# Four modulation rows computed by VectorE beside the first projections, and their own stage left out

## The reference, cut to what matters

```python
sh1, sc1, gt1, sh2, sc2, gt2 = split(silu(c) @ w_mod + b_mod, 6)
p = modulate(x, norm1_g, sh1, sc1) @ w_in          # first projections: q, k, v of the attention, and more
o_da = diff_attn(rope(q), rope(k), v)
o_gdn = gated delta rule, both directions
x_new = x + gt1 * (concat(o_da, o_gdn) @ w_out)
h = rms_norm(x_new, norm2_g) * (1 + sc2) + sh2      # router and experts work on h
x_new = x_new + gt2 * experts(h)
```

## Time and profile before

| | us |
|---|---|
| median of 3 runs | 4340.51 (4334.54 to 4346.90) |
| the profiled execution, its own time | 4332.25 |
| its span, first to last instruction | 4330.4 |
| TensorE (PE) busy | 3777.9 |
| VectorE (DVE) busy | 1570.3 |
| ScalarE (ACT) busy | 762.6 |
| GpSimd (POOL) busy | 310.4 |

### The profile page before, as it was taken

How to read it: one execution, slowest core, us unless ns; L and a number is a source line. 1 busy time by engine, 2 the same in 40 slices (tenths; PEclk the granted TensorE clock), 3 DMA queues, 4 the chain that set the end, 5 groups by cost and what they waited for, 6 DMA issues and landing times. The chain is left out here.

```text
span 4330.4 us, 32749 instructions
## 1 busy us (share of the span) xinstructions
PE 3777.9 (87%) x12890; PEld 1994.8 (46%) x12890; DVE 1570.3 (36%) x2513; ACT 762.6 (18%) x1409; POOL 310.4 (7%) x260
## 2 busy tenths in 40 slices
PE   7989989777798399999959476888888999999999
PEld 3446664446645144444435353344443444444444
DVE  3226634566413500000142617899812132121000
ACT  2014423333401000000020114122220110010000
POOL 0000000034200000000010000000000022121000
PEclk8999989888898699999979757889999999999999
DMA  5000000052352488888650101101122201110211
GB/s 180 20 21 1 1 2 29 30 133 58 122 195 78 172 337 320 313 322 312 243 187 0 12 10 52 39 22 30 37 92 97 97 30 49 39 49 20 83 58 44
DMA packets 193501, 425.97 MB, mean 98 GB/s; under 512 B 71648, under 2 KB 119936, under 8 KB 180672
## 3 DMA queue, kind: packets, MB, share of 16 engines
q1 hardware_dynamic: 183936, 392.57, 26.1%
q0 software_dynamic: 8272, 29.38, 2.3%
q10 hardware_dynamic: 1152, 2.10, 0.1%
HBM read 374.78 MB, written 48.05 MB: 98 GB/s over the span
## 5 line engine op out<-in xcount | busy, mean ns | idle before, releaser
L1728 PE MATMUL psum<-arena 128*128 128x512 f32 x1536 | 670.0, 594 | 2.9 <-DVE arena L1811 1.3
L2842 PE MATMUL psum<-arena 128*128 128x512 f32 x1232 | 532.4, 595 | 5.7 <-DVE arena L2900 4.1
L1728 PEld LDWEIGHTS psum<-arena 128*128 128x128 f32 x1536 | 289.4, 190 | 360.8 <-issue 357.8
L2842 PEld LDWEIGHTS psum<-arena 128*128 128x128 f32 x1232 | 234.7, 191 | 302.8 <-issue 294.6
L2498 PE MATMUL psum<-arena 128*128 128x512 f32 x512 | 264.6, 664 | 75.1 <-ACT arena L2571 75.0
L2969 PE MATMUL psum<-arena 128*128 128x512 f32 x704 | 305.0, 596 | 7.9 <-DMA arena<-in_w_ffn_down_dram 7.5
L2969 PEld LDWEIGHTS psum<-arena 128*128 128x128 f32 x704 | 133.8, 190 | 179.0 <-issue 170.6
L677 PE MATMUL psum<-arena 128*128 128x512 f32 (+1 forms) x512 | 202.2, 551 | 1.1 <-PEq L396 1.1
L2498 PEld LDWEIGHTS psum<-arena 128*128 128x128 f32 x512 | 102.4, 211 | 213.5 <-issue 189.7
L2610 DVE MAX8 arena<-arena 128x8 f32<-128x1024 f32 (+5 forms) x192 | 171.2, 892 | 4.7
L2612 DVE MATCH_REPLACE8 arena<-arena 128x1024 f32<-128x1024 f32 (+5 forms) x192 | 168.5, 878 | 0.0
(11 more groups left out here) (456 smaller groups left out, 4642.1 us busy)
## 6 DMA issues: line engine op xcount, KB each, us to landing
arena<-in_w_gate_dram SPq DMA_DIRECT2D x32, 2048.0 KB, 7.3
arena<-in_w_up_dram SPq DMA_DIRECT2D x32, 2048.0 KB, 8.8
arena<-in_w_down_dram SPq DMA_DIRECT2D x32, 2048.0 KB, 7.9
arena<-in_w_mod_dram SPq DMA_DIRECT2D x12, 2048.0 KB, 12.3
arena<-gd_rows SPq DMA_DIRECT2D x56, 256.0 KB, 4.2
arena<-in_w_ffn_gate_dram SPq DMA_DIRECT2D x11, 1024.0 KB, 5.5
arena<-in_w_ffn_up_dram SPq DMA_DIRECT2D x11, 1024.0 KB, 5.3
arena<-in_w_ffn_down_dram SPq DMA_DIRECT2D x22, 512.0 KB, 3.7
```

Of the source, the lines that this page charges most:

```text
L1728: ins = nc.tensor.matmul(ps[:, banks + j, :], lhs[:, k], W[n][:, h, k % 4, j * 512:(j + 1) * 512], start=(k == 0), stop=(k == KD - 1))
L2842: ins = nc.tensor.matmul(out(q), left[:, k], right[:, k], start=first and k == 0, stop=last and k == 3, skip_group_check=not first)
```

## The change

The eight chunks of the four rows are computed in stage_da_project. SyncE loads w_mod's chunks there into a ring of two (w_rows). After each rotary step r VectorE runs row_part(r): four of the eight 128x512 slices of chunk r // 2, each multiplied by its column of silu_c and added into acc (one tensor_scalar or scalar_tensor_tensor each). The sum over the 128 partitions is left to TensorE: row_sum(c), one product of acc with a matrix of ones, into bank 6 or 7, right after the swap of step 2c + 3 (the last one before the last task). VectorE copies one partition of it (row_out), and SyncE stores it as 2 KB in DRAM (mod_rows). stage_gdn_out now loads the four rows (2 MB), their biases (2 MB) and norm2_g (0.5 MB) as broadcasts to 128 partitions after the gate, and then w_out; GpSimd adds the biases and makes the scale row, in three operations of 4096, 1024 and 1024 elements a partition. stage_rows is dropped from the list.

```diff
--- before.py
+++ after.py
@@ -286,6 +286,11 @@
     raw = A.take("raw", 3, 512)
     tmp = A.take("rope_tmp", 2, 512)
     w_in = e.in_["w_in"][0].rearrange("(k p) n -> p k n", p=P)
+    NC = 8
+    wm, acc, row = A.take("w_rows", 2, KD, 512), A.take("row_acc", 2, 512), A.take("row_out", 2, 512)
+    w_mod = e.in_["w_mod"][0].rearrange("(k p) n -> p k n", p=P)
+    e.rows_dram, e.s_rowst = nc.dram_tensor("mod_rows", (4, D), F32).ap(), [e.keep_sem(f"dap_rowst{i}") for i in range(2)]
+    s_wm, s_acc, s_part, s_rmm, s_rev = [e.sem(f"dap_wm{i}") for i in range(2)], *(e.sem(f"dap_{n}") for n in ("acc", "part", "rmm", "rev"))
     tasks = []
     for m in range(DAH):
         tasks += [("q", 0, m, s, n) for s, n in TOKEN_RANGES[1:]]
@@ -300,8 +305,18 @@
         @block.sync
         def _(sp):
             sp.dma_start(rope, e.in_["rope"].rearrange("p (a n) -> p a n", a=2)).then_inc(s_rope, 16)
-            sp.wait_ge(s_mm, last_of[0] + 1)
-            sp.dma_start(w[:, 0], w_in[:, :, 1024:1536]).then_inc(s_w[0], 16)
+            for c in range(NC + 2):
+                if c < NC:
+                    if c >= 2:
+                        sp.wait_ge(s_acc, c - 1)
+                    sp.dma_start(wm[:, c % 2], w_mod[:, :, 2 * D + 512 * c:2 * D + 512 * c + 512]).then_inc(s_wm[c % 2], 16)
+                if c == 4:
+                    sp.wait_ge(s_mm, last_of[0] + 1)
+                    sp.dma_start(w[:, 0], w_in[:, :, 1024:1536]).then_inc(s_w[0], 16)
+                if c >= 2:
+                    d = c - 2
+                    sp.wait_ge(s_rev, d + 1)
+                    sp.dma_start(e.rows_dram[d // 2:d // 2 + 1, 512 * (d % 2):512 * (d % 2) + 512], row[0:1, d % 2]).then_inc(e.s_rowst[d % 2], 16)
 
         @block.tensor
         def _(pe):
@@ -310,6 +325,12 @@
                 if r >= 2:
                     pe.wait_ge(s_done, r - 1)
                 nc.tensor.matmul(e.ps[:, 4 + r % 2, :], e.const("swap"), raw[:, r % 3], start=True, stop=True).then_inc(s_swap, 1)
+
+            def row_sum(c):
+                pe.wait_ge(s_acc, c + 1)
+                if c >= 2:
+                    pe.wait_ge(s_rev, c - 1)
+                nc.tensor.matmul(e.ps[:, 6 + c % 2, :], e.const("ones"), acc[:, c % 2], start=True, stop=True).then_inc(s_rmm, 1)
 
             done = 0
             for i, (kind, c, m, s, n) in enumerate(tasks):
@@ -327,10 +348,11 @@
                 ins.then_inc(s_mm, 1)
                 while done < len(roped) and roped[done] < i:
                     swap(done)
+                    if done % 2 and done >= 3:
+                        row_sum(done // 2 - 1)
                     done += 1
-            while done < len(roped):
-                swap(done)
-                done += 1
+                if i == len(tasks) - 2:
+                    row_sum(NC - 1)
 
         @block.scalar
         def _(act):
@@ -349,7 +371,31 @@
 
         @block.vector
         def _(dve):
-            step = Steps(dve, s_own)
+            part = Steps(dve, s_part)
+
+            def row_part(r):
+                c, half = divmod(r, 2)
+                if half == 0:
+                    dve.wait_ge(s_wm[c % 2], 16 * (c // 2 + 1))
+                    if c >= 2:
+                        dve.wait_ge(s_rmm, c - 1)
+                for k in range(4 * half, 4 * half + 4):
+                    f = e.silu_c[:, k, 0:1]
+                    if k == 0:
+                        part(nc.vector.tensor_scalar(acc[:, c % 2], wm[:, c % 2, k], f, None, ALU.mult))
+                    else:
+                        ins = nc.vector.scalar_tensor_tensor(out=acc[:, c % 2], in0=wm[:, c % 2, k], scalar=f, in1=acc[:, c % 2], op0=ALU.mult, op1=ALU.add)
+                        if k < KD - 1:
+                            part(ins)
+                        else:
+                            ins.then_inc(s_acc, 1)
+
+            def row_out(c):
+                dve.wait_ge(s_rmm, c + 1)
+                if c >= 2:
+                    dve.wait_ge(e.s_rowst[c % 2], 16 * (c // 2))
+                nc.vector.tensor_copy(row[0:1, c % 2], e.ps[0:1, 6 + c % 2, :]).then_inc(s_rev, 1)
+
             dve.wait_ge(s_rope, 16)
             for r, i in enumerate(roped):
                 kind, c, m, s, n = tasks[i]
@@ -361,8 +407,12 @@
                 nc.vector.tensor_tensor(tmp[:, 1], e.ps[:, 4 + r % 2, :], rope[:, 1, o:o + n], ALU.mult).then_inc(s_own, 1)
                 dve.wait_ge(s_own, 2 * r + 2)
                 nc.vector.tensor_tensor(dst, tmp[:, 0], tmp[:, 1], ALU.add).then_inc(s_done, 1)
+                row_part(r)
+                if r % 2 and r >= 3:
+                    row_out(r // 2 - 1)
                 dve.wait_ge(s_done, r + 1)
-    A.give("w_da", "rope", "raw", "rope_tmp")
+            row_out(NC - 1)
+    A.give("w_da", "rope", "raw", "rope_tmp", "w_rows", "row_acc", "row_out", "silu_c")
 
 
 
@@ -1343,7 +1393,9 @@
     e.catB = A.take("catB", GH, L)
     gate = A.take("gate", GH, L)
     gn = A.take("gdn_norm", 1)
-    e.w_rows, e.s_wrows = A.take("w_rows", 3, KD, 512, high=True), [e.keep_sem(f"mr_w{i}") for i in range(3)]
+    e.rows, bm, g2 = A.take("rows", 4, D), A.take("b_rows", 4, D), A.take("norm2", D)
+    e.w_o, e.s_wo = A.take("w_o", KD, D, high=True), e.keep_sem("or_wo")
+    s_rows, s_pown = e.sem("go_rows"), e.sem("go_pown")
     sq = A.take("gsq", 2, GH * GD)
     ss = A.take("gss", TL, GH)
     s_in, s_gate, s_sq, s_ss, s_rt, s_own, s_y, s_tr, s_silu, s_ev = (
@@ -1355,10 +1407,20 @@
             sp.dma_start(gate, e.gate_dram.rearrange("h p n -> p h n")).then_inc(s_gate, 16)
             with nc.allow_non_contiguous_dma("gain by channel"):
                 sp.dma_start(gn, e.in_["gdn_norm_g"][0].rearrange("(p a) -> p a", a=1)).then_inc(s_in, 16)
-            w_mod = e.in_["w_mod"][0].rearrange("(k p) n -> p k n", p=P)
-            for c in range(3):
-                at = 2 * D + c * 512
-                sp.dma_start(e.w_rows[:, c], w_mod[:, :, at:at + 512]).then_inc(e.s_wrows[c], 16)
+            for i in range(2):
+                sp.wait_ge(e.s_rowst[i], 64)
+            sp.dma_start(e.rows, e.rows_dram.partition_broadcast(P)).then_inc(s_rows, 16)
+            sp.dma_start(bm.rearrange("p a n -> p (a n)"), broadcast_rows(e.in_["b_mod"][0, 2 * D:6 * D])).then_inc(s_rows, 16)
+            sp.dma_start(g2, broadcast_rows(e.in_["norm2_g"][0])).then_inc(s_rows, 16)
+            sp.dma_start(e.w_o, e.in_["w_out"][0].rearrange("(k p) n -> p k n", p=P)).then_inc(e.s_wo, 16)
+
+        @block.gpsimd
+        def _(pool):
+            own = Steps(pool, s_pown)
+            pool.wait_ge(s_rows, 48)
+            own(nc.gpsimd.tensor_tensor(e.rows, e.rows, bm, ALU.add))
+            own(nc.gpsimd.tensor_scalar(e.rows[:, 2], e.rows[:, 2], 1.0, None, ALU.add))
+            own(nc.gpsimd.tensor_tensor(e.rows[:, 2], e.rows[:, 2], g2, ALU.mult))
 
         @block.scalar
         def _(act):
@@ -1410,60 +1472,7 @@
                 for h in range(GH):
                     ins = nc.tensor.transpose(e.ps[:, t % 4, h * P:(h + 1) * P], e.og(t)[:, h * P:(h + 1) * P], e.ident)
                 ins.then_inc(s_tr, 1)
-    A.give("gate", "gdn_norm", "gsq", "gss", "f_Y")
-
-
-
-def stage_rows(e):
...
-    A.give("w_rows", "b_row", "norm2", "silu_c")
+    A.give("gate", "gdn_norm", "gsq", "gss", "f_Y", "b_rows", "norm2")
 
 
 
@@ -2987,7 +2996,7 @@
     A.give("w_ring", "o_ring", "hid", "x4")
 
 
-STAGES = [stage_entry, stage_da_project, stage_da, stage_gdn_project, stage_gdn, stage_gdn_out, stage_rows,
+STAGES = [stage_entry, stage_da_project, stage_da, stage_gdn_project, stage_gdn, stage_gdn_out,
           stage_out_router, stage_choose, stage_experts, stage_between, stage_project2,
           stage_ssm, stage_glu, stage_heads, stage_sparse,
           stage_merge, stage_out2, stage_ffn_up, stage_ffn_down]
```

More of the change, by code:

```diff
@@ L1412, in _ @@
                 ins.then_inc(s_tr, 1)
-    A.give("gate", "gdn_norm", "gsq", "gss", "f_Y")
-def stage_rows(e):
-    nc, A = e.nc, e.arena
-    e.rows = A.take("rows", 4, D)
-    w, s_w = e.w_rows, e.s_wrows
-    bm = A.take("b_row", 2, 512)
-    g2 = A.take("norm2", D)
-    e.w_o, e.s_wo = A.take("w_o", KD, D), e.keep_sem("or_wo")
-    w_mod = e.in_["w_mod"][0].rearrange("(k p) n -> p k n", p=P)
-    s_b = [e.sem(f"mr_b{i}") for i in range(2)]
-    s_in, s_mm, s_row, s_own = (e.sem(f"mr_{n}") for n in ("in", "mm", "row", "own"))
-    NC = 8
-    with nc.Block() as block:
-        @block.sync
-        def _(sp):
-            for c in range(NC):
-                if c >= 3:
-                    sp.wait_ge(s_mm, c - 2)
-                at = 2 * D + c * 512
-                if c >= 3:
-                    sp.dma_start(w[:, c % 3], w_mod[:, :, at:at + 512]).then_inc(s_w[c % 3], 16)
-                if c >= 2:
-                    sp.wait_ge(s_row, c - 1)
-                sp.dma_start(bm[:, c % 2], broadcast_rows(e.in_["b_mod"][0, at:at + 512])).then_inc(s_b[c % 2], 16)
-            sp.dma_start(g2, broadcast_rows(e.in_["norm2_g"][0])).then_inc(s_in, 16)
```

(22 more changed lines are left out.)

## The result

| | before | after |
|---|---|---|
| median of 4 runs, us | 4337.83 (4334.54 to 4346.90) | 4303.66 (4297.77 to 4308.74) |
| profiled execution, its own time | 4332.25 | 4297.77 |
| its span | 4330.4 | 4295.9 |

The ratio is 0.9917 (95% interval 0.9896 to 0.9939): 34.2 us faster by the medians, where 35.7 was forecast. The profiled executions differ by 34.5 us.

What follows compares the result with a forecast made beforehand. TensorE, busy 87% of the span, and stage-end barriers were taken as the bound. Router stage 42.6 us earlier less 6.9 for eight products gives 35.7; 4340.5 - 35.7 = 4305 us, range 4300 to 4313, plus 6 either way for run spread.

Steps and rivals of the forecast that it cites:

- What is removed: Dropped rows stage: its whole stretch from 1185.89 to 1245.36, 59.47 us, leaves the path.
- The router's start behind the longer pause: Router stage: it started at the lower clock already, so the longer pause costs nothing new.
- The eight products: First projections, TensorE: eight products of ones at 0.86 us each add 6.9 us, all on the path.
- VectorE: First projections: a rotary step needs 5.8 of 7.72 us, idle before L361 falls from 5.58 to some 2; nobody stands.
- Weights: First projections: eight 2 MB loads beside the projections cost nothing, covered by 20.3 us from issue to need.
- rival 3: First projections: VectorE waits for weights, rotary steps and TensorE wait behind it; slower, 4354 us, chance 0.04.
- Loads ahead of POOL: Stage before the router: 4.72 MB of broadcasts at 300 GB/s take 15.7 us, bounds 12.4 to 22.2, landing at 1189.2.
- the rule that I weighed: Stage before the router: DMAs of 128 partitions and at least 1 MiB reach maximum bandwidth; loads would end 3.3 us earlier.
- rival 1: Stage before the router, everything at its quick bound, broadcasts as fast as plain loads: gain 39.9, 4301 us, chance 0.2.
- POOL: Stage before the router: three finishing operations of 9.4, 1.3 and 2.4 us, sum 13.1, bounds 12.2 and 14.7.
- The stage: Stage before the router: ends at 1202.3, router begins at 1202.8; w_out lands by 1199.3 to 1201, inside POOL's 13 us.
- What the sum missed: Whole kernel: the sum held only the router stage 42.6 us earlier less 6.9 in the first projections, gain 35.7.

Runs made afterwards that it cites:

- add_only: Kernel before plus only the new work in the first projections, its own stage for the rows kept; 4349.8 us, first projections 215.82 us.
- shift8: Kernel before plus eight products of ones in the first projections, read by nobody, nothing else of the change; delta rule stage 295.10 us.
- parts_x3: Kernel after with every group of four VectorE parts issued three times; first projections 239.48 us, 23.8 more than after.
- dve_finish: Kernel after with biases and scale row finished on VectorE in place of POOL; 4302.1 us in one execution, stage before the router 26.72 us.
- experiment 4: Four kernels on the kernel before: four, eight or sixteen unread products, or a DRAM tensor with eight stores; delta rule 290.6 to 295.1 us with products, 288.16 with stores.

## Why the prediction was right

- **What is removed**: the stage of 59.47 us is gone whole; the number is the kernel before's own, and the router stage now follows the bordering one directly. The router's start behind the longer pause was no slower: TensorE's first product to the stage's end took 160.88 us against 162.48.
- **The eight products**: 6.9 forecast; 6.71 after, 6.89 in add_only, 6.64 in shift8, which has them without the rest. All of it on the path.
- **VectorE**: covered, as argued; slack 2.7 to 3.0 us where I said some 2. parts_x3 shows that this slack is the cover. The point where it decides is row_sum's wait, for which the prediction had said that nobody stands; with three times the parts it was the first to be late.
- **Weights**: landed in 7.8 to 14.7 us (10 to 13 forecast, 20.3 allowed); VectorE never waited for them, so nothing of rival 3 came.
- **Loads ahead of POOL**: the term that I had sized too high. 4.72 MB took 12.7 us after the gate's landing (1186.5 to 1199.2), 372 GB/s, where I took 300 and the bounds were 12.4 to 22.2. The nearest rows, 213 and 276 for broadcasts of 512 and 256 KB, misled: the window moved 403 GB/s in all at a share of 0.98, like the plain loads' 395. Here the rule that I weighed, of "DMA: Bandwidth & Descriptors" in the Trainium skill, section "Rules for kernel authors" (128 partitions and at least 1 MiB for the maximum), was the better guide: it gave 3.3 us less, 3.0 were measured. This is rival 1's mechanism, and it came true in the loads alone.
- **POOL**: 8.81, 2.78 and 2.34 us against 9.4, 1.3 and 2.4. tensor_scalar took over twice the forecast and longer than the tensor_tensor of its size. The Trainium skill ("GPSIMD Engine Reference", "Engine selection") has one-input operations on GpSimd roughly at line-rate; the measurement decides, and 2.78 us is 3.7 times VectorE's 0.756 for a tensor_scalar of 1024 elements. With the gaps the sum was 14.1, forecast 13.1. (The prediction's bounds for the sum, 12.2 and 14.7, come to 12.4 and 14.5 from its own terms.)
- **The stage**: 35.53 us, forecast 37.15; w_out under POOL's cover, as said, and next late once POOL is gone (dve_finish).
- **What the sum missed**: the delta rule's 6.09 us. The prediction had no step for it: it took the stages between for unchanged because their code is. The traces in experiment 4 put 3.9 us of loss to VectorE's steps stretched beside POOL's; the rest stays open. Against the 6.09 stand 1.6 us of the bordering stage, forecast too long, 0.2 of the products, and 3.0 from the router on, which lie within what two profiles of one kernel differ by (1.3 in the router stage, 2.4 in the experts'). So the sum of the change's own parts was -37.5 in fact, -35.7 in the forecast, and the whole hit within 1.5 us with an error of 6 in it that smaller ones paid back. The closeness is luck; the mechanism and the large terms are not. The delta rule's stage alone moved by up to 10.1 us in the kernels tried, so the same reasoning could have missed by that.

## What to carry to other kernels

A product with 128 equal columns spends TensorE's time on copying a vector; where VectorE has slack beside a bound stage, it can do the sum over the other axis, and TensorE adds the partitions once: 64 products became 8. What remains on the path afterwards is how the result comes back, so finish it while it is small (one row) and load it behind what the next stage needs first, which shortened this border by another 14 us in the profiles (198.81 to 184.74). Before trusting a difference below 0.3% in a kernel with stages that wait on chains of small steps, compare stage by stage, put the same delay into the kernel before, and look for the first place in the stage's timeline where the two part.

## What the runs showed of the hardware that was not expected

The delta rule's length hangs on the program, but not on its own code: 285.0 to 295.1 us over 14 profiles of 12 kernels, and within 0.3 us for the two kernels that were profiled twice. The router stage moves in the same way: from TensorE's first product to its end it took 160.3 to 166.4 us, with the same 128 products. Two things in the rows answer to where the work falls in time. One is the clock: TensorE paused and came back at half of it. In the kernel before:

```profile
955.00:960.00 5.00, 1.89 (x11) 1.12 (x9) 3.34 (x13) 0.60 (x1) 2.66 (x1) 1.00 0.78 267
960.00:965.00 5.00, 0.00 (x0) 0.00 (x0) 4.66 (x13) 0.00 (x0) 0.00 (x0) 0.70 0.81 119
965.00:970.00 5.00, 0.65 (x32) 0.54 (x32) 3.99 (x10) 0.48 (x2) 0.00 (x0) 0.50 0.97 137
```

The other is larger here: VectorE's small operations take three to four times as long while POOL has one running. In the kernel before, the 64x168 step and the next ones ran ahead of POOL's first operation, and TensorE waited 1.93 us for L1303:

```profile
1031.34 0.33 DVE L1266 TENSOR_TENSOR arena<-arena 64x168 f32<-64x168 f32 x1
...
1032.79 1.27 POOL L997 TENSOR_TENSOR arena<-arena 128x512 f32<-128x512 f32 x1 [9.29 <-DMA arena<-gd_rows]
1032.82 1.29 DVE L1303 TENSOR_TENSOR arena<-arena,psum 128x512 f32<-128x512 f32 x2
...
1033.66 3.65 PE L1127 MATMUL psum<-arena 128*128 128x128 f32 x16 [1.93 <-DVE arena L1303]
```

In the kernel after, the same step fell into it and took as long as POOL's, with three more behind it, and TensorE waited 5.96 us for the same operation (L1353 here):

```profile
1040.88 1.29 POOL L1047 TENSOR_TENSOR arena<-arena 128x512 f32<-128x512 f32 x1 [7.63 <-DMA arena<-gd_rows]
1041.09 1.26 DVE L1316 TENSOR_TENSOR arena<-arena 64x168 f32<-64x168 f32 x1
1042.13 1.34 POOL L1057 TENSOR_TENSOR arena<-arena 128x512 f32<-128x512 f32 x1
1042.39 1.27 DVE L1317 TENSOR_TENSOR arena<-arena 64x168 f32<-64x168 f32 x1
...
1046.34 1.29 DVE L1353 TENSOR_TENSOR arena<-arena,psum 128x512 f32<-128x512 f32 x2
...
1047.18 3.56 PE L1177 MATMUL psum<-arena 128*128 128x128 f32 x16 [5.96 <-DVE arena L1353]
```

The Trainium skill, "SBUF — State Buffer", section "SBUF: two separate sides", has the two engines share one pair of ports, taken whole for an instruction's length, and a VectorE operation with two operands in SBUF needs it against a GpSimd operation that reads SBUF; the rows agree, 1.26 us against 0.33, while L1303, with one operand in PSUM, took 1.29 us for two beside POOL's L997 and was not stretched. VectorE's total in the stage hardly differs (160.25 and 159.92 us; 19 and 20 long steps in the whole stage), so it is the place of the long steps in the chain that changes, not their number: in the kernel before they come behind L1303, where they hold up nothing: the next group of products (L1135, in the kernel after L1185) is 6.9 us later in the kernel after, as much as L1303. For this change it means that the finishing operations on POOL stretched nothing: they began at 1199.26, when VectorE's last operation of the stage had ended at 1198.4.
